# A convolution unit inside the recurrence, and two joins: one change to a fused block kernel on one core

## The reference

```python
h = rms_norm(x, pre_norm_w)
p_rwkv, p_conv, p_pool, p_gate = split(h @ w_in)          # widths 2176, 2048, 1024, 3072
y_a = rwkv7_branch(token_shift(p_rwkv, mu), ...)          # recurrence over time, then a group norm, times silu(z)
b, c, u, z = split(p_conv, 4)                             # short_conv_branch
y_b = b * causal_conv3(c * u) * silu(z)
y_c = pool_branch(p_pool, ...)
proj = einsum('nbsc,ncd->nbsd', stack([y_a, y_b, y_c]), w_branch)
merged = sum_n(sigmoid(gate_n) * proj_n)
x = x + rms_norm(merged @ w_out, post_norm_w)
```

## Time and profile before

| what | value |
|---|---|
| median of 3 runs | 1404.14 us (1403.64 to 1405.38) |
| the profiled execution | 1405.23 us, of it the span 1403.5 us |
| TensorE matmuls | 1383.0 us busy (99%) |
| VectorE | 795.0 us (57%) |
| ScalarE | 700.9 us (50%) |
| GpSimd | 798.7 us (57%) |
| granted TensorE clock | 1.000 |
| recurrence, four chunks | 917 to 1013.2 us |
| its tail | 1013.2 to 1026.5 us |
| convolution stage behind the tail | 1026.5 to 1111.2 us |
| pool units | 1111.2 to 1158.1 us |
| branch steps | 1158.1 to 1347.5 us |
| last product and end | 1347.5 to 1403.5 us |

### The profile page before, as it was taken

One profiled execution on the slowest core, in us unless ns is written; L12 is line 12 of the kernel. 1 busy time (PEld: TensorE's weight loads), 2 busy tenths in 40 slices (PEclk: granted clock), 3 DMA queues, 4 the chain that ended last, 5 costly groups with the idle time before them and its releaser, 6 DMA issues.

```text
span 1403.5 us, 24701 instructions
## 1 busy us (share of the span) xinstructions
PE 1383.0 (99%) x9656; PEld 1166.6 (83%) x9656; DVE 795.0 (57%) x970; ACT 700.9 (50%) x1215; POOL 798.7 (57%) x599
## 2 busy tenths in 40 slices
PE   9999999999999999999999999999999999999998
PEld 6888888787889888888888887788888788999987
DVE  5566665547646433433544776634459866867732
ACT  6555555536436544444422369555555434445543
POOL 4444444257336666666665465964356865766782
PEclk9999999999999999999999999999999999999999
DMA  5222222122131222323233312210013222333232
GB/s 212 91 90 76 83 83 76 65 100 91 61 122 59 67 100 91 103 90 105 94 104 115 113 49 98 75 33 4 4 64 131 90 90 91 106 106 104 91 105 75
DMA packets 34222, 123.04 MB, mean 88 GB/s; under 512 B 3792, under 2 KB 4304, under 8 KB 34000
## 3 DMA queue, kind: packets, MB, share of 16 engines
q1 hardware_dynamic: 33408, 119.51, 25.1%
q10 hardware_dynamic: 720, 2.20, 0.4%
HBM read 119.59 MB, written 2.10 MB: 87 GB/s over the span
## 4 chain that ended last, share of the span: by engine, by line
PE 81%; DVE 10%; issue 4%; ACT 3%; POOL 2%; DMA 0%; SPq 0%; POOLq 0%; ACTq 0%; DVEq 0%
PE ps L589 16%; PE ps L590 15%; PE ps L591 15%; PE ps L1456 3%; PE ps L1458 3%; PE ps L1457 3%; PE ps L1524 1%; PE ps L1525 1%; PE ps L1526 1%; PE ps L711 1%; PE ps L696 1%; PE ps L724 1%; POOL w_lo L2261 1%; PE ps L1151 1%; DVE t_val L3068 1%
## 5 line engine op out<-in xcount | busy, mean ns | idle before, releaser
L2261 POOL TENSOR_TENSOR w_lo<-stage,w_hi 128x512 fp32r<-128x512 f32 x378 | 561.1, 1509 | 387.5 <-ACT w_hi L1555 387.2
L589 PE MATMUL ps<-x_hi,w_lo 128*128 128x512 f32 x712 | 281.2, 395 | 0.8 <-POOL w_lo L2261 0.8
L591 PE MATMUL ps<-x_hi,w_hi 128*128 128x512 f32 x712 | 277.5, 390 | 0.0
L590 PE MATMUL ps<-x_lo,w_hi 128*128 128x512 f32 x712 | 277.4, 390 | 0.0
L1555 ACT ACTIVATE w_hi<-stage 128x512 fp32r<-128x512 f32 x378 | 216.3, 622 | 57.3 <-DMA stage<-w 44.1
L589 PEld LDWEIGHTS ps<-x_hi,w_lo 128*128 128x128 f32 x712 | 133.7, 188 | 32.1 <-issue 2.6
L591 PEld LDWEIGHTS ps<-x_hi,w_hi 128*128 128x128 f32 x712 | 133.7, 188 | 28.1
L590 PEld LDWEIGHTS ps<-x_lo,w_hi 128*128 128x128 f32 x712 | 133.8, 188 | 27.5 <-issue 1.0
L2773 DVE SCALAR_TENSOR_TENSOR conv<-ps,vcol,conv 128x511 f32<-128x511 f32 x44 | 33.0, 749 | 132.8 <-ACT conv L1775 132.8
L2445 POOL TENSOR_TENSOR w_lo<-stage,w_hi 128x512 fp32r<-128x512 f32 x44 | 75.4, 1742 | 54.0 <-DVE s_val L3139 54.0
L1775 ACT ACTIVATE conv<-ps,vcol 128x512 f32<-128x512 f32 x44 | 34.2, 778 | 121.4 <-PE ps L591 120.4
(11 more groups left out here) (532 smaller groups left out, 3473.0 us busy)
## 6 DMA issues: line engine op xcount, KB each, us to landing
stage<-w SPq DMA_DIRECT2D x211, 512.0 KB, 3.2
extra_stage<-w SPq DMA_DIRECT2D x6, 512.0 KB, 5.0
H<-xT SPq DMA_DIRECT2D x4, 512.0 KB, 7.5
mem<-memT SPq DMA_DIRECT2D x2, 512.0 KB, 10.8
pool_n<-pool_count ACTq DMA_DIRECT2D x1, 1024.0 KB, 5.3
outT<-outs SPq DMA_DIRECT2D x4, 256.0 KB, 2.0
outT<-outs SPq DMA_DIRECT2D x2, 384.0 KB, 2.7
w_small<-small ACTq DMA_DIRECT2D x1, 512.0 KB, 6.5
```

The lines of the kernel that those rows point to most:

```text
L589: pe.matmul(out, wl, hi(k), start=first, stop=False)
L590: pe.matmul(out, wh, lo(k), start=False, stop=False)
L591: mm = pe.matmul(out, wh, hi(k), start=False, stop=end)
L2261: pool.tensor_tensor(unit_lo(b)[:, cols], unit_stage(b)[:, cols], unit_hi(b)[:, cols].bitcast(F32), ALU.subtract).then_inc(wlo_made, 1)
```

## The change

Each chunk of the recurrence takes in two blocks of convolution unit 0: in chunks 0 to 2 one in front of level 5 and one behind it, in chunk 3 one in front of level 4 and one in front of level 5. The unit goes to bank 3, which is free because both groups' transposed products now share bank 2; TensorE therefore waits for both groups' transposed updates. The blocks that stand in the tail are now those of unit 1 and of unit 2's start, and they wait for both updates of the last level. The head sums stand two blocks earlier behind y_product (twelve blocks instead of fourteen between them). The split of unit 3 moves into chunk 1, and the splits behind it move up by one.

The first join: at the start of the pool stage ScalarE waits for the convolution's third tile only, splits pool unit 2, and takes the last tile between the first two pool units; GpSimd takes its low part one unit later. The second join: in the last product tiles 2 and 5 use bank 2, a tile waits for the one three before it, and unit 3 is split ahead of the tiles.

```diff
@@ names
+        def OUT_BANK(t):
+            return (U0["out"] + (0, 1, 0, 0, 1, 0, 0, 1)[t]) % 2 if t not in (2, 5) else 2
+        def turned_cols(g, h):
+            return slice((4 * (1 - g) + h) * HB, (4 * (1 - g) + h + 1) * HB)
+        def CONV_BANK(j):
+            return j % 4 if j else 3
@@ TensorE, tile() of the last product
-                    pe.wait_ge(evac, t + (EV0[n] + CREDIT - 1))
+                    if t > 2:
+                        pe.wait_ge(evac, t - 2 + (EV0[n] + CREDIT))
...
-                product(ps[:, 6 if t == 2 and n != "out" else (u + (n == "wo")) % 2, :], u, u % RING, hi, lo, between=between)
+                bank = OUT_BANK(t) if n == "out" else 6 if t == 2 else (u + (n == "wo")) % 2
+                product(ps[:, bank, :], u, u % RING, hi, lo, between=between)
@@ TensorE, level()
-                        pe.wait_ge(ch_tt_s, 2 * ((NL - 1) * c + l - 2) + g + 1)
+                        pe.wait_ge(ch_tt_s, 2 * ((NL - 1) * c + l - 2) + 2)
...
-                            mm = pe.matmul(ps[half(d), 2 + g, cols], R, T, start=True, stop=True)
+                            mm = pe.matmul(ps[half(d), 2, turned_cols(g, h)], R, T, start=True, stop=True)
@@ TensorE, conv_blocks()
-                if j >= 4 and k0 == 0:
-                    pe.wait_ge(evac, EV0["conv"] + j - 3 + CREDIT)
+                if j >= 3 and k0 == 0:
+                    pe.wait_ge(evac, EV0["conv"] + max(j - 3, 1) + CREDIT)
...
-                    o = ps[:, j % 4, :]
+                    o = ps[:, CONV_BANK(j), :]
@@ TensorE, the order
             for c in range(NS):
                 for l in range(1, NL + 1):
+                    if l == NL and c < NS - 1:
+                        conv_blocks(0, 2 * c, 2 * c + 1)
+                    if l >= NL - 1 and c == NS - 1:
+                        conv_blocks(0, 3 + l - 1, 4 + l - 1)
                     level(c, l)
                 if c < NS - 1:
+                    conv_blocks(0, 2 * c + 1, 2 * c + 2)
                     for g in range(2):
                         turned_x(c + 1, g)
                 if c == NS - 1:
-                    pe.wait_ge(ch_xt_s, 2 * NL * NS - 1)
-                    conv_blocks(0, 0, 2)
+                    pe.wait_ge(ch_xt_s, 2 * NL * NS)
+                    conv_blocks(1, 0, 2)
                 corner_first(c)
             right_side(NS - 1)
-            conv_blocks(0, 2, 4)
+            conv_blocks(1, 2, 4)
             corner(NS - 1)
             right_side_turned(NS - 1)
-            conv_blocks(0, 4, 6)
+            conv_blocks(1, 4, 6)
             sa_product(NS - 1)
-            conv_blocks(0, 6, 8)
-            conv_blocks(1, 0, 2)
+            conv_blocks(1, 6, 8)
+            conv_blocks(2, 0, 2)
             y_product(NS - 1)
-            conv_blocks(1, 2, 8)
+            conv_blocks(2, 2, 6)
...
-            conv_blocks(2, 0, 8)
+            conv_blocks(2, 6, 8)
+            conv_blocks(3, 0, 6)
...
             head_sums(y_hi, y_lo)
-            conv_blocks(3, 0, 4)
+            conv_blocks(3, 6, 8)
+            conv_blocks(4, 0, 2)
...
             head_sums(sq_hi, sq_lo)
-            conv_blocks(3, 4, 8)
-            for j in range(4, 16):
+            conv_blocks(4, 2, 8)
+            for j in range(5, 16):
                 conv_blocks(j, 0, 8)
@@ ScalarE
-                    if c == 0 and l == 2:
-                        split_hi(U0["conv"] + 2)
+                    if c < 2 and l == 2:
+                        split_hi(U0["conv"] + 2 + c)
...
-            split_hi(U0["conv"] + 3)
+            split_hi(U0["conv"] + 4)
             conv_taken(1)
...
-            split_hi(U0["conv"] + 4)
+            split_hi(U0["conv"] + 5)
...
             conv_taken(2)
-            split_hi(U0["conv"] + 5)
             split_hi(U0["conv"] + 6)
...
-            conv_hi(CA - 1)
-            act.wait_ge(cv_lo_s, CA)
+            act.wait_ge(cv_lo_s, CA - 1)
...
             for j in range(CA):
+                if j == 1:
+                    act.wait_ge(cv_lo_s, CA)
...
                     split_hi(b + 2)
+                    if j == 0 and c == 1:
+                        conv_hi(CA - 1)
...
             split_hi(U0["out"] + 2)
+            split_hi(U0["out"] + 3)
...
-                if b + AHEAD < UNITS:
+                if j and b + AHEAD < UNITS:
                     split_hi(b + AHEAD)
@@ GpSimd
-                    if c == 0 and l == 4:
-                        split_lo(U0["conv"] + 2)
+                    if c < 2 and l == 4:
+                        split_lo(U0["conv"] + 2 + c)
...
             for j in range(16):
-                split_lo(U0["conv"] + AHEAD + j)
+                if j:
+                    split_lo(U0["conv"] + AHEAD + j)
...
-                if j == 14:
+                if j == 15:
                     conv_lo(CA - 1)
@@ VectorE, update_turned()
-                    dve.tensor_tensor(T, T, ps[:, 2 + g, 4 * HB:8 * HB], ALU.add).then_inc(ch_tt_s, 1)
+                    dve.tensor_tensor(T, T, ps[:, 2, 4 * HB * (1 - g):4 * HB * (2 - g)], ALU.add).then_inc(ch_tt_s, 1)
```

More of the change, by code:

```diff
@@ L2063, in conv_taken @@
                 if c < 3:
-                    act.activation(cb[:, t % 2, c, :], ps[:, j % 4, :], ACT.Copy).then_inc(evac, 1)
+                    act.activation(cb[:, t % 2, c, :], ps[:, CONV_BANK(j), :], ACT.Copy).then_inc(evac, 1)
                 else:
-                    act.activation(sg[:, t % 2, :], ps[:, j % 4, :], ACT.Silu).then_inc(evac, 1)
+                    act.activation(sg[:, t % 2, :], ps[:, CONV_BANK(j), :], ACT.Silu).then_inc(evac, 1)
             def conv_hi(t):
@@ L2227, in _ @@
                 act.wait_ge(acc2_made, j + BEFORE["acc2_made"]["out"])
-                act.activation(sqv[:, j % 2, :], ps[:, b % 2, :], ACT.Square).then_inc(sq_made, 1)
-                act.activation(Y[:, j, :], ps[:, b % 2, :], ACT.Identity, scale=V("post", j)).then_inc(evac, 1)
-                if b + AHEAD < UNITS:
+                act.activation(sqv[:, j % 2, :], ps[:, OUT_BANK(j), :], ACT.Square).then_inc(sq_made, 1)
+                act.activation(Y[:, j, :], ps[:, OUT_BANK(j), :], ACT.Identity, scale=V("post", j)).then_inc(evac, 1)
+                if j and b + AHEAD < UNITS:
                     split_hi(b + AHEAD)
@@ L3002, in update_turned @@
                     ins = dve.tensor_tensor(TF[rows, 4 * g:4 * g + 4, HB * d:HB * d + HB], XT[rows, c % 2, g, 1, :, :],
-                                            ps[rows, 2 + g, 4 * HB:8 * HB].rearrange("p (h n) -> p h n", n=HB), ALU.add)
+                                            ps[rows, 2, 4 * HB * (1 - g):4 * HB * (2 - g)].rearrange("p (h n) -> p h n", n=HB), ALU.add)
                 ins.then_inc(ch_tf_s, 1)
```

## The result

| comparison | changed kernel | before | ratio, 95% interval |
|---|---|---|---|
| 15 runs each | 1406.79 us (1404.77 to 1410.7) | 1404.64 us (1403.38 to 1407.2) | 1.0014 (1.0008 to 1.0021) |

The change costs about 2.1 us (by the interval 1.1 to 2.9). So it is no gain, and about as small as the 0.2% that the prediction drew as its bound: 0.85 us were forecast in the other direction, and 1406.79 lies above the range's 1405.8. The profiled execution took 1405.61 us, its span 1403.9. Its mean granted clock was 0.999; of the 15 runs two showed 1.000 (1405.19 and 1405.24 us), the others 0.998 or 0.999, and the seven at 0.998 all took 1406.7 us or more.

A forecast was written before the change was run, and what follows sets the result against it. It took TensorE and a group norm chain through VectorE, ScalarE and GpSimd to bound the convolution stage at once. Terms +2.4 - 1.3 - 0.3 - 0.9 - 0.75 = -0.85 us gave a median of 1403.3 us, range 1401.8 to 1405.0.

The forecast's parts named there:

- Which bound holds at unit 12: Convolution unit 12: TensorE catches up with the chain ending in GpSimd's w_lo and waits 4 us for it.
- Behind T: Behind T, the first convolution block after the last y_product: only the chain's shift counts; stage ends at +2.4 - 1.6 = +0.8.
- The chain: Group norm's chain from g_mu to unit 12's low half: 1.3 us earlier against T, plus 0.3 of relief.
- the relief: VectorE's norm steps meet two GpSimd unit splits instead of three: 0.3 us taken, between none and 1.5.
- rival of port relief: VectorE and GpSimd slow each other; one split less gives back 1.5 us, sum -2.1, 1402.0 us; chance 0.11.
- The recurrence: Blocks in chunks 0 to 2, in chunk 3 and the tail delay T by 0.6 + 1.3 + 0.5 = +2.4 us.
- the tail: Tail blocks in bank 1 wait for group 1's update too, up to y_product: +0.47 us.
- The rival of blocks that cost in full: Each of eight blocks delays the recurrence by 0.91 us; sum +4.5, 1408.6 us; chance 0.07.
- Both groups in bank 2: Recurrence levels: waiting for both transposed updates costs 0, as ScalarE's R copy ends later; up to 0.4 a level otherwise.
- The joins: Stalls at pool unit 2 and at tile 2 of the last product go: -0.9 and -0.75 us.
- Full pay: Convolution stage: unit 12 does not wait, so the stage gives 5.46 us; sum -4.7, 1399.4 us; chance 0.16.

The follow-up runs named there:

- runs with 14 and 7 added matmuls: Changed kernel with 14 or 7 matmuls nobody reads filling TensorE's time ahead of unit 12's wait; 1404.27 us, ratio 1.0003, and 1404.64 us, ratio 0.9996.
- joins alone: Kernel before with only the pool join and the join of the last product; 1403.0 us, ratio 0.9994.
- no blocks: Changed kernel with group norm's low part, ScalarE's splits and last tile's low part reordered, but no convolution blocks in the recurrence; 1402.58 us, ratio 0.9977.
- the new order: Changed kernel, group norm's low part behind unit 15's split, ScalarE's splits earlier: ratio 0.9989; last tile's low and high parts later too: 1399.01 us, 0.9959.

## Why the prediction was wrong

The mechanism was right up to unit 12: the blocks made TensorE wait there for GpSimd. What the wait costs was wrong, and three smaller terms were off.

**Which bound holds at unit 12: right.** Unit 12 waited for w_lo, from 1086.60 to 1090.04, and unit 10 for 1.45: 4.9 us, for 4 forecast with some 0.5 at unit 10. Moving one GpSimd instruction took the wait at unit 12 away.

**The step that failed** is the last one of the part "Behind T": "Of the 8 x 0.68 = 5.46 us taken out of this stage only the chain's own shift counts: the stage ends at +2.4 - 1.6 = +0.8 against before." A wait of 4 us was costed as if TensorE went on at full speed behind it. It went on at 1.2 GHz for eight matmuls, +1.57 us, a term that the prediction did not have. The runs with 14 and 7 added matmuls show this term by itself, 1.63 and 1.67. Counted from the first R product, the stage ends 3.65 us later than before (1113.54 - 918.23 against 1111.23 - 919.57), and not 0.8. The Trainium skill (TensorE: Matmul & The Clock Gate, "Part 1: The HAM clock gate") says that the array's clock is gated by how busy the engine has been, at 1.2 GHz when idle and 2.4 GHz when busy. By that rule the forecast wait was itself a warning; this trace agrees, with 0.50 behind the wait at unit 12.

**The chain: too short by 0.57.** From the first block behind y_product to unit 12's low half it is 1090.04 - 1028.25 = 61.79 us for 62.82 before: 1.03 less, not 1.6. The head sums start 8.29 us behind T (8.2 forecast), and g_mu 10.30 instead of 11.67, the whole 1.37. What is missing is the relief, put at 0.3: VectorE's first step took 2.70 us instead of 2.29, and the second 3.27 as before. Relief there was, further on, and more than the 1.5 us of the rival: with GpSimd's splits over, two steps of VectorE's first convolution tile took 1.17 us instead of 3.19 (the rows at 1050 and 1051 us). It bought nothing. The tile's last step waits for ScalarE's sg, which stands behind the norm's Ln and Exp, and that wait grew from 0.47 to 2.50 us. So the rival of port relief fails by the path and not by the size: the chain passes through ScalarE at that point, and time saved on VectorE ahead of it does not count.

**The recurrence: +3.06 and +2.89 instead of +2.4.** By chunk the blocks cost 0.32, 0.33 and 0.32 in chunks 0 to 2 (0.6 forecast, 0.97 measured), 1.12 in chunk 3 (1.3), the tail 0.46 (0.47). The rest is 0.3 us in chunk 0 ahead of any block, at level 3, and 0.17 in chunk 2 of the first profile alone. The list of waits has there an "issue" of 0.2 in the changed kernel's profiles, and of 0.4 or 0.7 in three others with blocks. The joins alone and "no blocks", whose recurrence is that of the kernel before, lose the 0.3 too, so it is not the blocks. Why TensorE's own stream stops there stays open. The rival of blocks that cost in full falls: 8 x 0.91 would have been 7.3.

**Both groups in bank 2: right**, zero by the profile of it alone.

**The joins: right.** From the first pool product to the end of the span it is 1403.5 - 1111.23 = 292.27 before and 1403.9 - 1113.54 = 290.36 after: -1.91, for -1.65.

**The sum.** Measured 3.06 - 1.03 + 1.57 - 1.91 = +1.69 (S: +1.74), forecast -0.85. Of the 2.54 between, 1.57 are the clock, 0.66 the recurrence, 0.57 the chain, and the joins give 0.26 back. So without the half clock the change would have stood at +0.1: inside the range, but no gain either, and the two runs with the wait filled show just that (S 484.19 and 483.78, for 483.93 before). The prediction's own range, 1401.8 to 1405.0, is narrower than its terms: 1.3 - 1.6 - 1.65 and 4.0 - 1.6 on 1404.14 (the joins in full, and not at all) give 1402.2 to 1406.5, still without a term for the clock. Full pay, rejected as a forecast at 0.16, is the state that the new order reaches by hand: C falls from 84.70 to 78.56.

## What to carry to other kernels

Where two engines' chains end close together, moving work off the one turns into a wait for the other: follow what stands ahead of the releasing instruction in its engine's queue (here a low part of 5.57 us, which is not asked for before 1137 us), and move that in the same change. Price a forecast wait of TensorE with what the clock does behind it, and not as idle time alone; if the wait can't be removed, matmuls on spare data into a bank nobody reads won back 1.6 us here. When one wait is removed, read the next stage: twice running the gain stopped at an instruction that waited, with a needed one queued behind it. And time saved on one engine counts only if the chain stays on that engine: the next instruction that waits for another can take it all.

## What the runs showed beside

One VectorE instruction of 128x256 took 5.36 us (816.06 to 821.42) beside four GpSimd splits in a row, and 1.59 us where it seems to have got in behind the first, in two profiles of the same program. The Trainium skill (SBUF — State Buffer, "Who interferes with whom") says that the two engines contend for a shared port pair and that issue order decides who blocks; the trace agrees, and the length of four splits and a rest suggests that the loser can be passed over several times. On TensorE that chance was worth 1.13 us.

In the profiles of the joins alone, of the run with 14 and of "no blocks" TensorE waits 2.0 us for VectorE's mk_lo near 332 us, where the first profiles of the two kernels show no such wait; in the last two the granted clock of the window from 329 to 336 is 0.83 and 0.86, and the first R product stands at 921.21 and 922.24. So here a wait of 2.0 us was followed by the half clock in two of three profiles. Such accidents lie ahead of the recurrence and have nothing to do with the change; they fit with single runs of one kernel 4 to 6 us apart, though of the unprofiled runs only the mean clock is known. At this size of effect S was the better measure.
